# Moving step-size work, a PSUM evacuation and two cache transfers in a hybrid RWKV-7 / S5 / attention step

## The reference

```python
# layer 0: two mixers on one input projection
z = rms_norm(x, g_norm) @ p['w_in']                    # 1024 -> 2304
oa, shift_new, s_new = rwkv7_mix(z[..., :A_COLS], shift_prev, s_rwkv, p)
ob, hr, hi = s5_mix(z[..., A_COLS:], h_re, h_im, p)
y = x + jnp.concatenate([oa, ob], axis=-1) @ p['w_out']
# s5_mix: the discretisation
lam = lax.complex(jnp.minimum(lam_re, -1e-4), lam_im)
dt = jnp.exp(log_dt)[:, None]
lam_dt = lam * dt
lam_bar = jnp.exp(lam_dt)
b_bar = ((lam_bar - 1.0) / lam)[..., None] * b
...
# layer 1: sliding-window attention; queries and keys get an RMS norm per head
kf = jnp.concatenate([ck, k], axis=1)                  # cached keys of the samples
vf = jnp.concatenate([cv, v], axis=1)
s = jnp.einsum('bqkgd,bskd->bkgqs', q, kf) * SCALE     # then a softmax with a sink, and values
# every layer ends with
x + jnp.square(jax.nn.relu(rms_norm(x, g) @ w1)) @ w2
```

## Time and profile before

| | us |
|---|---|
| median of 3 runs | 1870.07 (1869.57 to 1871.56) |
| the profiled execution, its own time | 1865.31 |
| its span | 1863.6 |
| PE busy | 1668.2 (90%) |
| DVE busy | 736.3 (40%) |
| POOL busy | 594.7 (32%) |
| ACT busy | 301.8 (16%) |

### The profile page before, as it was taken

One profiled execution on the slowest core, in us unless ns is written; L12 is line 12 of the kernel. 1 busy time (PEld: TensorE's weight loads), 2 busy tenths in 40 slices (PEclk: granted clock), 3 DMA queues, 4 the chain that ended last, 5 costly groups with the idle time before them and its releaser, 6 DMA issues.

```text
span 1863.6 us, 33438 instructions
## 1 busy us (share of the span) xinstructions
PE 1668.2 (90%) x14584; PEld 1586.9 (85%) x14584; DVE 736.3 (40%) x1256; ACT 301.8 (16%) x487; POOL 594.7 (32%) x356
## 2 busy tenths in 40 slices
PE   5997876686868999999999999976799999999999
PEld 5996765575647899999999999974599999999999
DVE  5645676555645543310132112657433320022200
ACT  3001222212121322200021101123212110011100
POOL 2343245130310333433343333322123333433332
PEclk9997776887879899999999999985699999999999
DMA  7540000000001344444444444350034444444442
GB/s 284 164 151 22 8 17 22 8 9 7 9 13 31 125 147 158 135 138 159 155 135 158 152 142 135 136 158 1 2 113 136 151 149 151 135 158 158 142 157 96
DMA packets 41609, 201.58 MB, mean 108 GB/s; under 512 B 13888, under 2 KB 15040, under 8 KB 19008
## 3 DMA queue, kind: packets, MB, share of 16 engines
q1 hardware_dynamic: 19232, 96.89, 15.0%
q0 software_dynamic: 12528, 91.23, 14.8%
q10 hardware_dynamic: 9744, 11.88, 2.2%
HBM read 192.82 MB, written 6.37 MB: 107 GB/s over the span
## 4 chain that ended last, share of the span: by engine, by line
PE 65%; DVE 4%; issue 1%; ACT 1%; POOL 1%; ACTq 0%; DVEq 0%
PE PS L572 17%; PE PS L574 17%; PE PS L573 17%; PE PS L547 2%; PE PS L549 2%; PE PS L548 2%; PE PS L667 1%; POOL EE L503 1%; PE PS L1068 1%; PE PS L1095 0%; DVE EE L2138 0%; DVE HH L2005 0%; PE PS L650 0%; DVE SM L2144 0%; PE PS L820 0%
## 5 line engine op out<-in xcount | busy, mean ns | idle before, releaser
L397 POOL TENSOR_TENSOR WL<-WR,WH 128x2048 fp32r<-128x2048 f32 x87 | 403.3, 4635 | 458.3 <-DMA WH<-in_w 440.0
L572 PE MATMUL PS<-HH,WH 128*128 128x320 f32 x1344 | 417.3, 310 | 7.0 <-DVE Z L1520 5.3
L574 PE MATMUL PS<-HH,WL 128*128 128x320 f32 x1344 | 416.3, 310 | 0.0
L572 PE MATMUL PS<-XH,WH 128*128 128x320 f32 x1120 | 347.2, 310 | 0.4
L573 PE MATMUL PS<-XL,WH 128*128 128x320 f32 x1120 | 346.1, 309 | 0.0
L574 PE MATMUL PS<-XH,WL 128*128 128x320 f32 x1120 | 346.1, 309 | 0.0
L573 PE MATMUL PS<-HL,WH 128*128 128x320 f32 x896 | 276.9, 309 | 0.0
L572 PEld LDWEIGHTS PS<-HH,WH 128*128 128x128 f32 x1344 | 253.3, 188 | 8.8 <-DVE Z L1520 5.5
L574 PEld LDWEIGHTS PS<-HH,WL 128*128 128x128 f32 x1344 | 253.3, 188 | 0.0
L572 PEld LDWEIGHTS PS<-XH,WH 128*128 128x128 f32 x1120 | 210.2, 188 | 1.4 <-issue 1.1
L573 PEld LDWEIGHTS PS<-XL,WH 128*128 128x128 f32 x1120 | 210.2, 188 | 0.3
(11 more groups left out here) (392 smaller groups left out, 2317.2 us busy)
## 6 DMA issues: line engine op xcount, KB each, us to landing
WH<-in_w POOLq DMA_DIRECT2D x87, 1024.0 KB, 5.3
WR<-in_w SPq DMA_DIRECT2D x87, 1024.0 KB, 4.9
X<-in_xT SPq DMA_DIRECT2D x8, 320.0 KB, 10.6
out<-X ACTq DMA_DIRECT2D x8, 320.0 KB, 3.2
UR<-UF ACTq DMA_DIRECT2D x16, 80.0 KB, 4.2
UF<-UR SPq DMA_DIRECT2D x64, 20.0 KB, 1.8
WR<-in_wglu SPq DMA_DIRECT2D x1, 1024.0 KB, 5.3
S<-in_s ACTq DMA_DIRECT2D x4, 256.0 KB, 2.8
```

The costliest lines, as they stand in the source:

```text
L397: nc.gpsimd.tensor_tensor(WL[:, r], WR[:, r], WH[:, r].bitcast(F32), ALU.subtract).then_inc(w_split, 2)
L572: mm(out, wh[:, k, wc], xh[:, k, cols], start=(k == 0), stop=False)
L574: last = mm(out, wl[:, k, wc], xh[:, k, cols], start=False, stop=(k == kt - 1))
```

## The change

Three edits. The exp of the log step sizes goes in front of the first norm copy on ScalarE, and VectorE's first block of the constants in front of its first low half; the wait for the loads of B, C and the sample states goes to the block that reads B. No block is run between the first and the second evacuation. The two cache transfers are issued after the copies, after the root, and after the two stores of new keys and values.

```diff
@@ ScalarE, norm
                     if L == 0:
-                        act.wait_ge(x_in[k], 16)
                         if k == 0:
                             act.wait_ge(params_in, 16)
+                            fn(S5[:, 0], prm_cols("ldt"), ACT.Exp).then_inc(s5_fn, 1)
+                        act.wait_ge(x_in[k], 16)
@@ ScalarE
             def s5_scalars():
-                fn(S5[:, 0], prm_cols("ldt"), ACT.Exp).then_inc(s5_fn, 1)
                 act.wait_ge(s5_arg, 1)
@@ ScalarE, qkv
-                act.dma_start(KS[:, :, :, 0:CH], ckT).then_inc(cache_in, 16)
-                act.dma_start(VS[0:CH, :, :], cv).then_inc(cache_in, 16)
                 for n in range(NCH + NB):
...
                 fn(KN[:, :], PS[:, 4, 0:20], ACT.Sqrt, bias=prm_col("eps"), scale=1.0 / 64).then_inc(qk_rms, 1)
                 act.dma_start(o_kv[:, 0], KR[:, :, T - 256:T]).then_inc(stored, 16)
                 act.dma_start(o_kv[:, 1], VP[:, :, CH + T - 256:CH + T]).then_inc(stored, 16)
+                act.dma_start(KS[:, :, :, 0:CH], ckT).then_inc(cache_in, 16)
+                act.dma_start(VS[0:CH, :, :], cv).then_inc(cache_in, 16)
@@ VectorE
-            def in_stage():
-
-                steps = s5_scalars()
+            def in_stage(steps):
+
                 for u in range(2 * N_IN):
                     evac_in(u)
-                    for _ in range(2):
+                    for _ in range(2 if u else 0):
                         next(steps, None)
@@ VectorE, s5_scalars
                 s = [S5[:, i] for i in range(16)]
-                dve.wait_ge(s5_in, 32)
                 dve.wait_ge(s5_fn, 1)
...
                 yield
+                dve.wait_ge(s5_in, 32)
                 coef = [s[13].unsqueeze(2).broadcast_to((P, NPR5, 16)), s[14].unsqueeze(2).broadcast_to((P, NPR5, 16))]
@@ VectorE, main
+            steps = s5_scalars()
+            next(steps)
             for k in range(KT):
                 norm_low(0, 0, k)
             rstd(0)
-            in_stage()
+            in_stage(steps)
```

## The result

The changed kernel takes 1856.15 us, median of 8 runs (1846.53 to 1864.66), against 1870.74 for the kernel before, median of 8 runs (1867.75 to 1872.26). The ratio is 0.9925, 95% interval 0.9903 to 0.9947: 14.6 us faster, where 10.5 were forecast. The profiled execution of the changed kernel took 1860.21 us for a span of 1858.5, which is only 5.1 us under that of before.

The account below looks back on a forecast made before the run. TensorE was taken to bound the kernel, with two long stalls at the changed lines. 6.2 - 0.8 + 5.5 - 0.4 = 10.5 us took the median from 1870.1 to 1859.6; final range 1855.5 to 1865.5.

Parts of the forecast that it names:

- The start at no cost: Kernel start: the moved block (1.85 us) and exponential (under 0.9) hide in idle time; cost nothing, 2.7 us without cover.
- The stall before unit 3 goes whole, the weights are late next: Input stage: the 5.28 us stall vanishes, unit 4 waits 1.9 us for weights; last fourteen units start 6.2 us earlier.
- The clock term: Input stage: the new stall may lower TensorE's clock and cost 0 to 2.9 us; 0.8 us was taken.
- The later weight slots have room: Input stage: GpSimd's next split starts its transfer at 49.5 us; TensorE wants the result only at 63.6.
- The cache transfers, 5.5 us of held copies: Attention: without the transfer issues ahead, the first V copy starts at 1235.4 instead of 1240.94, 5.5 us earlier.
- The issue in its new place: Attention, behind root and stores: second issue takes about 6.20 us, bounded by 10.1 to landing; 0.4 us cost taken.
- rival (a): Attention: ScalarE is held in the new place longer than VectorE allows; time 1861.5 to 1864, chance 0.12.
- the case in which it asks for the exponentials sooner: Attention: L1019's broadcast at full clock asks up to 2.3 us sooner; ScalarE's late queue would swallow that gain.
- The attention term: Attention: 5.5 us from earlier V copies less 0.4 for the late issue; range 3 to 6.5 us.
- rival (b): Attention: the issue is not what held ScalarE, or V copies wait for something else; time 1864.7, chance 0.05.
- Rival (c): Input stage: evacuation 1 does not release unit 3, only attention pays; time 1865.0, chance 0.03.
- Rival (d), the clock in the long stretch: Small dependent steps, 200 to 300 us: clock 0.58 instead of 0.70 costs 15 us, time 1874.7; chance 0.10.

Follow-up runs that it names:

- swap_old: The kernel before with only the order of the two cache transfers exchanged, in their old place: 1863.36 us, ratio 0.9952.
- in_only: The kernel before with the two input-stage edits alone, cache transfers in their old place: 1863.32 us, ratio 0.9955.
- The halves: The kernel before with the input-stage edits alone (ratio 0.9955), and with the move of the cache transfers alone (1864.23 us, ratio 0.9959).
- copies_later: The changed kernel with ScalarE's two memory-to-memory cache copies issued in the S5 stage: 1855.09 us, ratio 0.9904.
- early_only: The kernel before with only the first block and its exponential moved to the start, two blocks still after unit 0: 1864.12 us, ratio 0.9956.
- pair_only: The kernel before with only no block after unit 0, so the two evacuations run back to back: 1867.13 us, ratio 0.9975.
- copies_later_old: The kernel before with ScalarE's two memory-to-memory cache copies issued in the S5 stage: 1872.22 us, ratio 1.0004.
- late_split_old: copies_later_old with GpSimd's subtraction for the third weight slot held until after evacuation 1: 1869.45 us, ratio 0.9996.

## Why the prediction was right, point by point
- **The start at no cost**: right. ScalarE's first copy even came at 5.63 us instead of 6.79, since its table load was done before the parameters landed. Before, the load began at 5.49, when they had landed. It bought nothing, since the first matmul waits for the weights at 16.0.
- **The stall before unit 3 goes whole, the weights are late next**: right, 1.64 us where 1.9 was worked out.
- **The clock term**: 0.8 us was taken from a range of 0 to 2.9. It was 0; the mean granted clock from 40.5 to 56 us was 1.00 after the stall of 1.64 us, where it had been 0.78 before.
- **"The later weight slots have room"**: wrong. The fourth slot's transfer was issued at 49.05 together with SyncE's next load and took 9.3 us, not 5.3, and the subtraction behind it took 5.54. TensorE waited 0.48 us there, and 2.4 in all three waits. This error and that on the clock cancel in part: 5.0 us were gained for 5.4 forecast. The nearness is luck.
- **The cache transfers, 5.5 us of held copies**: right, but the row of copies shrank as well, from 6.07 us (2.83 and 3.20 in its two groups) to 4.5. What differs is the clock at which TensorE feeds them: it had idled 7.4 us and fallen to the half level; now it did not fall. That the two transfers no longer run beside the copies isn't the reason: in swap_old they do, with the DMA engines full (share 1.15) and a granted clock of 1.00 from 1244 to 1246 us, and the two groups take 2.32 and 2.22 us. From 1236 to 1238 us, before and after (PE, PEld, DVE, ACT, POOL busy, granted clock, DMA share, GB/s):
```profile
1236.00:1238.00 2.00, 0.00 (x0) 0.00 (x0) 2.00 (x1) 0.00 (x0) 0.00 (x0) 0.50 1.05 416
```
```profile
1236.00:1238.00 2.00, 1.99 (x16) 0.88 (x14) 1.97 (x2) 1.98 (x8) 0.00 (x0) 1.00 0.80 320
```
  From the end of the last square to the root it takes 6.9 us and took 14.1, so 7.2 us were gained where 5.5 were put. The text had allowed 1 us either way.
- **The issue in its new place**: 8.16 us where 6.20 was taken, inside the bound of 10.1. Of rival (a) this much is true: the first exponential came 11.1 us after the root, where it had been 9.2 before, and cost VectorE 0.92 us where 0.4 was put. The broadcast behind the root ran at a granted clock of 0.50 as before, so the case in which it asks for the exponentials sooner did not arise. The attention term is 5.7 us for 5.1 forecast, again with two errors against each other.
- **The rule of the Trainium skill** ("DMA: Bandwidth & Descriptors", section "Issuing engines are not separate DMA queues") on short issue times, rival (b), did not hold for this row: 8.16 us of issue in the new place. With no short rows ahead the same issue took 0.56 us, as the rule would have it.
- **Rival (c)** is out by in_only, which gained 8.1 us.
- **Rival (d), the clock in the long stretch**: present as scatter; a loss is not shown. From the load behind the input stage to the last store of RWKV the span was 452.0 us in the first trace of before (155.29 to 607.28) and 456.2 in that of after (150.31 to 606.48), with a mean granted clock of 0.78 and 0.76 from 156 to 606. That took back 4.2 of the 10.7 us that the two stages gained in the profiled pair, and 1.4 us more went in scatter of the two long MLP stretches; so the pair differs by 5.1 only. Over the seven kernels with a changed input stage this stretch runs from 453.5 to 459.1, over the six with the old one from 452.0 to 455.1. The trace of before has the shortest of all thirteen; a small loss from the new entry is not excluded.
- **The sum.** The stages gave 5.0 + 5.7 = 10.7 us in the traces; the timed medians gave 14.6, with an interval of 9.9 to 18.1. The halves gave 8.1 (5.8 to 10.9) and 7.2 (4.5 to 10.9). The interval of both together holds the 10.7 and that of the attention half its 5.7, each in the lower part; that of the input half doesn't hold the 5.0 of the changed kernel's trace, and just misses the 5.7 of in_only's own. The step that was thin is the one that took the profiled execution for the kernel and carried its 4.8 us under the median along as a constant. Runs with the long stall of 9.5 us are one way in which the median of before can lie above that trace. The changed kernel had no such case in its trace, nor had copies_later with the subtraction at 40.52, since evacuation 1 starts right behind evacuation 0. One more pattern of the record fits this: the five kernels that leave attention as it was (in_only, early_only, pair_only, copies_later_old, late_split_old) all come out better against the timed runs of before than their last evacuation does against the 154.31 of its trace, by 2.2 to 3.1 us by the medians and 1.1 to 3.0 by the ratios. It is as if the timed runs of before ended their input stage that much later; an estimate from the 4.4 us between the ends of 154.31 and of 158.71 (swap_old) is that a quarter to two thirds of them would need the long stall. That it is so stays open.
- **The forecast's own numbers.** The measured 1856.15 lies in the range that the prediction ends on, 1855.5 to 1865.5, and 0.35 us under the narrower one of its sum, 1856.5 to 1864. The upper end of that one was added up wrongly: with the clock term at 2.9 and the attention term at 3 the gain is 6.3 us and the time 1863.8, not 1863.5. The two stages gave 10.7 us for 10.5 forecast, but by errors that cancel in each, so the agreement of the sum is partly luck; the mechanisms of both stages are what the traces bear out.
- **The signs it named.** The wait on the weights before unit 4, the subtraction near 44.9 (44.52), the first matmul near 15.9 and the copies right behind the square came as forecast. The first exponential was to start at 1248.2 and started at 1253.17: 4.7 us of that are the stretches in between, which this trace ran slower. One sign of being wrong came true, an issue longer than 8 us that VectorE's first sum waits for; it cost 0.92 us. The granted clock from 200 to 300 us was 0.66 where it had been 0.70, above the 0.6 that was named.

## What to carry to other kernels
When a stall is a chain of small instructions on VectorE, look where GpSimd's long elementwise instructions start: one trace shows one position only, and a subtraction that started 4 us sooner made the stall 9.5 us instead of 5.3. Release what another engine waits for first, and put fillers behind it. Issue a transfer made of short rows last in its queue, or where the issuing engine has nothing to do: moved in front of other work, the wait goes with it.

## What the runs showed of the hardware
- A VectorE instruction on 16 columns took 4.44 us (swap_old), 4.48 (copies_later_old) and 4.24 (copies_later) when it began while GpSimd's subtraction on SBUF ran; it ended with it. PSUM evacuations beside a subtraction kept their 0.49 us. The Trainium skill, "SBUF — State Buffer", section "Who interferes with whom", has this: VectorE with two SBUF inputs or in a 2-port mode and GpSimd exclude each other for a whole instruction, and one SBUF input outside those modes does not. The traces agree in the small products (two SBUF inputs) and in the evacuations (one). Two of the three held instructions above are tensor_scalar with one SBUF input; no row shows in which mode they ran.
- A DMA issue on ScalarE's queue took 6.1 to 8.2 us right behind the transfer of short rows (6.20 in the kernel before, 8.16 in the changed one, 6.09 in pair_only). With it out of the way the same issue took 0.56 us and those of the cache copies and stores 0.41 to 0.63; a store issued 8 us behind it took 1.26 (swap_old).
- Making a transfer of 1 MB land 4 us sooner (wait of 7.2 instead of 11.2 us on GpSimd, copies_later_old) made the kernel no faster: ratio 1.0004 (0.9992 to 1.0016).
- ScalarE's table load can run before the operand of the instruction that needs it is there: in the changed kernel it started at 2.46 us and the exponential at 5.50, when the parameters had landed. In the kernel before, with two waits ahead of the copy, it started at 5.49. Why it waited there no run shows.
